# Splitting q and k of a latent-attention encoder into hi and lo parts when they are projected, not when they are read back

## The reference

```python
h = rmsnorm(x, norm_mix)
qa, ka, va, ga, cq, ckv, kr, gb = split(h @ w_in)
ya = window_attention(qa, ka, va, sink) * silu(ga)      # 8 heads, |t-s| <= 128
q = rmsnorm(cq, q_a_norm) @ w_uq                        # 384 -> 8 heads x (64 nope + 32 rope)
kv = rmsnorm(ckv, kv_a_norm) @ w_ukv                    # 256 -> 8 heads x (64 k_nope + 64 v)
q_rope, k_rope = apply_rope(q[..., 64:]), apply_rope(kr)   # k_rope is shared by the heads
scores = (q_nope . k_nope + q_rope . k_rope) * 96 ** -0.5
yb = softmax(scores) @ v * silu(gb)                     # dense, 8 heads, 1024 x 1024
out = rmsnorm(x + concat(ya, yb) @ w_out, final_norm)
```

## Time and profile before

| | |
|---|---|
| median of 3 runs | 620.34 us (619.05 to 620.73) |
| the profiled execution | 619.11 us |
| its span in the trace | 617.3 us |
| PE busy | 605.8 us (98%) |
| weight loads busy | 494.8 us (80%) |
| DVE, ACT, POOL busy | 452.2, 358.4, 320.8 us |
| DMA | 86.36 MB, mean 140 GB/s |
| clock granted to PE, mean over the span | 0.996 |

### The profile page before, as it was taken

One profiled execution on the slowest core, in us unless ns is written; L12 is line 12 of the kernel. 1 busy time (PEld: TensorE's weight loads), 2 busy tenths in 40 slices (PEclk: granted clock), 3 DMA queues, 4 the chain that ended last, 5 costly groups with the idle time before them and its releaser, 6 DMA issues.

```text
span 617.3 us, 9331 instructions
## 1 busy us (share of the span) xinstructions
PE 605.8 (98%) x3180; PEld 494.8 (80%) x3180; DVE 452.2 (73%) x863; ACT 358.4 (58%) x762; POOL 320.8 (52%) x303
## 2 busy tenths in 40 slices
PE   8999998999999999999999999999999999999996
PEld 7888886888888888888887777777777777888885
DVE  5774862534444439989999798988989898789684
ACT  6643431223333228778886787878787788633563
POOL 4611604404656532535537777886887789510701
PEclk9999998999999999999999999999999999999999
DMA  7696457385776620101006633324323423499043
GB/s 252 187 282 210 127 171 252 136 295 170 237 252 227 221 68 2 35 2 35 1 27 152 199 89 74 70 65 90 77 61 78 103 85 138 159 349 343 1 153 121
DMA packets 59089, 86.36 MB, mean 140 GB/s; under 512 B 6617, under 2 KB 32737, under 8 KB 58913
## 3 DMA queue, kind: packets, MB, share of 16 engines
q1 hardware_dynamic: 58880, 85.48, 44.9%
q10 hardware_dynamic: 160, 0.27, 0.1%
HBM read 51.26 MB, written 24.77 MB: 123 GB/s over the span
## 4 chain that ended last, share of the span: by engine, by line
PE 82%; DMA 6%; DVE 5%; ACT 2%; SPq 1%; issue 1%; POOL 1%; DVEq 0%; ACTq 0%
PE ps L1662 14%; PE ps L1664 14%; PE ps L1663 14%; PE ps L1932 10%; PE ps L1950 5%; PE ps L1949 5%; PE ps L1869 5%; PE ps L1864 5%; PE ps L1834 3%; PE ps L1884 2%; DMA lat_scratch<-lat_b 2%; PE ps L1844 2%; DMA x_in<-x 2%; PE ps L1821 2%; PE ps L1820 2%; PE ps L1845 1%
## 5 line engine op out<-in xcount | busy, mean ns | idle before, releaser
L1516 DVE TENSOR_TENSOR pT_lo<-ps,pT_hi 128x512 fp32r<-128x512 f32 x128 | 88.2, 691 | 16.4 <-ACT pT_hi L1105 16.4
L1105 ACT ACTIVATE pT_hi<-ps 128x512 fp32r<-128x512 f32 x128 | 76.0, 596 | 37.0 <-PE ps L1932 36.7
L810 POOL TENSOR_SCALAR p_b<-p_b,stat 128x1024 f32<-128x1024 f32 x64 | 71.9, 1124 | 36.6 <-DVE stat L1511 36.6
L1662 PE MATMUL ps<-hT_hi,w_hi 128*128 128x512 f32 x208 | 84.0, 404 | 0.0
L1664 PE MATMUL ps<-hT_hi,w_lo 128*128 128x512 f32 x208 | 81.4, 391 | 0.0
L1663 PE MATMUL ps<-hT_lo,w_hi 128*128 128x512 f32 x208 | 81.1, 390 | 0.0
L1932 PE MATMUL ps<-ident,p_b 128*128 128x128 f32 x512 | 78.1, 275 | 0.2
L1506 DVE TENSOR_REDUCE stat<-ps 128x1 f32<-128x1024 f32 x64 | 77.7, 1215 | 0.7 <-PE ps L1884 0.6
L1932 PEld LDWEIGHTS ps<-ident,p_b 128*128 128x128 f32 x512 | 60.9, 140 | 21.2 <-issue 7.8
L1094 ACT ACTIVATE p_b<-ps,stat 128x1024 f32<-128x1024 f32 x64 | 71.2, 1113 | 6.4 <-DVE stat L1506 2.5
L1949 PE MATMUL ps<-pT_hi,vB 128*128 128x512 f32 x128 | 55.3, 432 | 0.0
(11 more groups left out here) (219 smaller groups left out, 1476.7 us busy)
## 6 DMA issues: line engine op xcount, KB each, us to landing
w_raw<-w_in SPq DMA_DIRECT2D x13, 512.0 KB, 4.7
x_in<-x SPq DMA_DIRECT2D x8, 512.0 KB, 3.9
wt_raw<-w_out SPq DMA_DIRECT2D x8, 512.0 KB, 4.3
t_scratch<-wt_hi SPq DMA_DIRECT2D x16, 256.0 KB, 2.5
t_scratch<-wt_lo SPq DMA_DIRECT2D x16, 256.0 KB, 2.8
q<-q_h SPq DMA_DIRECT2D x16, 256.0 KB, 3.7
wn_raw<-w_in SPq DMA_DIRECT2D x8, 336.0 KB, 3.7
lat_scratch<-lat_b SPq DMA_DIRECT2D x32, 80.0 KB, 2.2
```

What stands on the lines that cost most here:

```text
L810: nc.gpsimd.tensor_scalar(p_b[:, (U + 1) % 4, :], p_b[:, (U + 1) % 4, :], r_b[:, U % 4:U % 4 + 1], 0.5, ALU.mult, ALU.mult).then_inc(s_bp, 1)
L1105: nc.scalar.activation(pT_hi[:, 1 - G % 2, 4 * a:4 * a + 4, U % 4 * P:(U % 4 + 1) * P], ps[:, 4 + a, :].rearrange("p (k c) -> p k c", c=P) ...
L1516: nc.vector.tensor_tensor(pT_lo[at_], ps[:, 4 + a, :].rearrange("p (k c) -> p k c", c=P), f(pT_hi[at_]), ALU.subtract).then_inc(s_bTl, 1)
L1662: nc.tensor.matmul(o, a_hi, b_hi, start=first, stop=False, skip_group_check=goes_on)
```

## The change

- **Up projections.** Every job but v now has two copies: ACT writes `stage` (hi), DVE writes `stage_lo` (lo = value minus hi), and SP stores both to separate halves of the scratch tensors. The jobs kr take four DMAs, since their rows are also interleaved. `s_upd` counts the lo copies, in the order of the jobs, and it is what the later job of the same bank waits for. The rope jobs r write their products and sums into `r_tmp`; ACT takes hi from there and DVE lo. `stage_lo[2]` and `stage_lo[3]` lie over `lat_b`, so DVE waits there for the last latents' store.
- **Last latents.** `rope_k` now takes blocks 0 to 4 after block 5, and 5 to 7 after block 7; ACT waits for it before block 6's square. Only the first half of `r_q` is loaded ahead of the last trip, the other half after `ukv_raw`.
- **Dense attention.** SP loads hi and lo rows from DRAM straight into `q_1`, `q_2`, `k_1`, `k_2`, `q_c` and `k_c`. All splits of q and k on POOL and DVE, and all copies of rows within SBUF, are gone; POOL still splits v. Loads of head h wait until head h-2 has been scored.
- `sums_wt(0)` on POOL waits until all stores of the up projections have landed, since `wt_sum` lies over `stage_lo`.

Cut to its core:

```diff
-        stage = at("stage", 89, [P, 4, HALF])
+        stage = at("stage", 89, [P, 4, HALF], F32R)
+        stage_lo = [at(f"stage_lo{i}", kb, [P, HALF], F32R) for i, kb in enumerate((113, 205, 142.5, 144.5))]
...
         def wait_up_copied(eng, j):
...
+            eng.wait_ge(s_upd, j + 1)
+        def stored(i, j):
+            dmas = {"kr": 4, "v": 1}
+            return 16 * sum(dmas.get(UP[k][0], 2) for k in range(i, j, 4))
...
-            sp.dma_start(r_q[:, :, :], rope_q).then_inc(s_rq, 16)
+            sp.dma_start(r_q[:, :, 0:HALF], rope_q[:, :, 0:HALF]).then_inc(s_rq, 16)
             move_lat(NT - 1)
             sp.dma_start(ukv_raw[:, :, :, :],
                          w_ukv.rearrange("(k p) (h c) -> p k h c", p=P, c=P)).then_inc(s_ukvi, 16)
+            sp.dma_start(r_q[:, :, HALF:SEQ], rope_q[:, :, HALF:SEQ]).then_inc(s_ukvi, 16)
...
+                for part in range(1 if kind == "v" else 2):
+                    if part == 0 and kind != "v":
+                        sp.wait_ge(s_upa, hi_count(j))
+                    else:
+                        sp.wait_ge(s_upd, j + 1)
+                    src = f(stage[:, j % 4, :] if part == 0 else stage_lo[j % 4][:, :])
...
+            sp.wait_ge(s_ws, REP * (W_UNITS - 1))
+            load_q(0, s_qk0)
...
+            load_k(0, s_qk0)
             sp.dma_start(v_raw[:, :, 0:HD], v_all[:, :, 0:HD]).then_inc(s_v0, 16)
...
+            load_q_c(0, s_qc0)
+            load_q(1, s_qk[1])
+            load_k(1, s_qk[1])
...
             for h in range(2, HEADS):
-                load_qk(h)
-                copy_rows(h)
+                sp.wait_ge(s_bs, NT * (h - 1))
+                load_q(h, s_qk[h % 2])
+                load_k(h, s_qk[h % 2])
+                load_q_c(h, s_qk[h % 2])
...
-                if t == NT - 2:
+                if t == NT - 3:
                     dve.wait_ge(s_small, 32)
-                    rope_k(slice(0, NT - 2))
-            rope_k(slice(NT - 2, NT))
+                    rope_k(slice(0, NT - 3))
+            rope_k(slice(NT - 3, NT))
             lat_lo(NT - 2)
             lat_lo(NT - 1)
...
-                    nc.vector.tensor_tensor(stage[:, (j - 1) % 4, :], r_tmp[:, 0, :], r_tmp[:, 1, :],
-                                            ALU.subtract)
...
+                    for i in (j - 1, j):
+                        dve.wait_ge(s_upa, hi_count(i))
+                        wait_slot(dve, i)
+                        nc.vector.tensor_tensor(stage_lo[i % 4][:, :], r_tmp[:, 2 * (i - j + 1), :], f(stage[:, i % 4, :]),
+                                                ALU.subtract).then_inc(s_upd, 1)
...
+                    if kind == "q":
+                        nc.vector.scalar_tensor_tensor(out=lo, in0=raw, scalar=B_SCALE, in1=hi, op0=ALU.mult,
+                                                       op1=ALU.subtract).then_inc(s_upd, 1)
+                    else:
+                        nc.vector.tensor_tensor(lo, raw, hi, ALU.subtract).then_inc(s_upd, 1)
```

More of the change, by code:

```diff
@@ new lines, in load_k @@
+            def load_k(h, done):
+                hp, rows = h % 2, slice(h * HD, (h + 1) * HD)
+                sp.dma_start(f(k_1[0:HD, hp, :]), k_scr[0, rows, :]).then_inc(done, 16)
+                for part in range(2):
+                    sp.dma_start(f(k_2[HD * (1 - part):HD * (2 - part), hp, :]), k_scr[part, rows, :]).then_inc(done, 16)
+                if h < 2:
+                    for i in range(2):
+                        sp.dma_start(f(k_1[HD + i * ROPE:QK + i * ROPE, hp, :]),
+                                     kr_scr[0].rearrange("p t c -> (p t) c")).then_inc(done, 16)
```

266 lines of the change are left out of this document (91 added, 175 removed).

## The result

The changed kernel takes 627.35 us (median of 4 runs, 625.72 to 629.03), the kernel before 620.34 (619.05 to 620.73): a ratio of 1.011, 95% interval 1.009 to 1.014. It is slower by 7 us. The forecast was 622.8 with a range of 617.5 to 626.0: the direction was right, the size was not. The profiled execution of the changed kernel took 625.72 us with a span of 623.8, against a span of 617.3 before: 6.5 us more.

A forecast was written before the change was run, and what follows sets the result against it. PE, busy 98% of the span, was taken as the bound. Stores +1.7, clock +1.8 and dense start -0.35 summed to +3.15 us, the latents' -0.85 being used up; forecast 622.8 us, between 622.3 and 623.5, range 617.5 to 626.

The forecast's parts named there:

- the start of the dense attention: Dense attention's start: PE's 0.35 us wait for POOL behind the head 0 split goes, -0.35 us.
- the time at which the stores of the second rotated pair begin: Up projections: the second rope pair's first hi part was put at 119.0, after a gap in the stores.
- The removed work in the dense attention: Dense attention: POOL's dropped splits and copies lie beside a PE with a regular period, so 0 us gained.
- so by about 332 … I count no wait: Dense start: head 0's k loads land by about 332, PE needs them at 335.74; q_c lands by 336.
- The last latents: Before job 8: a shorter store-to-load trip, 4.6 us, starts job 8 at 98.5, not 99.35: -0.85 us.
- The doubled stores: At `gated(0)`: 14.5 MB queued ahead delay job 28's copy, so it starts at 137.1, not 135.39: +1.7 us.
- The clock: Behind the wait at `gated(0)`: PE's idle time brings one stretch at 1.2 GHz, +1.8 us.
- The one ending faster: Up projections: stores keep up at 390 GB/s without a gap, `gated(0)` starts 2.7 us earlier, 617.3; chance 0.17.
- a sign of being wrong: Stores: the forecast is wrong if they move at 390 GB/s.
- The rival with waits in more places: Stores at 340 GB/s, `q_c` of head 0 late, or stretched rope pairs making jobs 12 and 20 wait: 626; chance 0.13.

The follow-up runs named there:

- the freed trip alone: Kernel before with half of the rope table's load put behind the weights and k's rotation one tile earlier, nothing else: 621.3 us, ratio 1.002.
- The old-trip run: Changed kernel with the whole rope table again ahead of the last latents' load and k's rotation one tile later: 628.12 us, ratio 1.014.
- the run with v first: Changed kernel with the load of v for the first dense head issued ahead of the five k loads: 625.68 us, ratio 1.009.
- the last version with turns: Changed kernel with last v jobs' banks moved, v loaded first, rotated-q banks freed early, and k and v jobs taking turns: 620.76 us, ratio 1.0013.
- the run with other banks: Changed kernel with the last two v jobs of the up projections in PSUM banks 0 and 1, not 6 and 7: 622.08 us, ratio 1.004.

## Why the prediction was wrong

**The mechanism was the forecast's, two terms of its sum were not.** It gave +3.15 us; the trace has +6.5. The steps that failed are the start of the dense attention, which came out 2.05 us dearer, and the time at which the stores of the second rotated pair begin, which came 1.5 us later.

- *The removed work in the dense attention, 0.* Right. From the first dense scores to the end both traces have 281.5 us, with 56 us less on POOL.
- *The start of the dense attention, -0.35.* Wrong, by 2.05 us. PE's wait for POOL did go, and the step "so by about 332 … I count no wait" looked at k and q_c alone. The step left out that v of head 0, the first load on SP in the earlier trace rows, now stands behind five loads of k, and that ACT's hi part of v stands ahead of the copies that PE's last window products need. It cost +1.70 over the stretch, 1.47 of which came back with one line moved. The rule for each moved step (what is queued behind it, and who waits for that) had been applied to k and not to what k was put in front of.
- *The last latents, -0.85.* Half right, and used up as forecast. Job 8 started at 99.04, not 98.5 (99.35 before). The trip took 5.39 us from store to load (88.33 to 93.72), not the 4.6 taken as a middle. One trace does not settle this: with half of the rope table ahead the trip took 3.2 to 5.8 us in the traces here, with all of it 4.8 to 5.9. Counted from the first up projection the latents' load was issued at 10.6 us here (9.7 to 11.6 in the traces with the new trip) and at 11.7 before (10.8 to 12.5 with the old one), which is near the gain forecast. In the kernel before, the freed trip alone won nothing (ratio 1.002, interval from 1.000 to 1.004); its trace has the first stores later by 1.4 us. The bounds were added up slightly wrong: 88.8 + 3.95 + 4.63 is 97.4, not 97.2, and nothing hangs on it.
- *The doubled stores, +1.7.* The term that decided, right in kind and too small: +3.2. PE came to `gated(0)` at 135.12 and waited 3.47 us, for a v copy behind stores, as the working had it. The first store of the second rotated pair came at 120.47, not 119.0, and from there on the working holds: `gated(0)` comes 18.1 us later in both, at 137.1 and at 138.59. So the 1.5 us lie ahead of that store, and the rows name two causes. One is the pair itself: DVE's products for it began only at 115.94, behind the lo part of job 11, whose hi part had waited for a store of a job kr, and the first sum took 1.33 us, not 0.69. The other is the bytes ahead. At 374 GB/s they were to be gone by 117.5; they kept the engines busy until 120.2, because 106 to 116 ran at 309 GB/s only. There SP takes 3.7 us (109.69 to 113.37) to issue the eight stores of the jobs kr, of 32 KB each, and the share falls to 0.35 at 112 to 114. The sum had counted the bytes of kr and not its eight issues. Since the gap was still there, but only some 1 us long (120.3 to 121.3), an earlier pair alone would have won at most this 1 us. No run here changes the stores of kr, so how much of the 1.5 us is theirs stays open. The old-trip run shows that the pair is the point that counts: the wait was 3.45 us there too, with job 20 at 124.81, 3.6 us later.
- *The clock, +1.8.* Right: +1.68, and gone with spare matmuls in the wait. That the clock held behind job 8 in the profiled execution was luck: it did so after a wait of 2.62 us, and in the run with v first it fell in both places. Two of the changed kernel's four runs took 629 us at a mean clock of 0.992 to 0.994 and two 625.7 at 0.996 to 0.997, which fits a second stretch in the longer ones. But a stretch is worth 1.7 us and the runs are 3.2 apart, and only one of the four has a trace, so the rest of that difference stays open.
- *The rivals.* The one ending faster asked for 390 GB/s without a gap. That rate came over 126 to 136 and was named as a sign of being wrong; it was not one, because the average over 96 to 136 was 343. DMA: Bandwidth & Descriptors of the Trainium skill measured 425 GB/s for 16 MB on one core; no 10 us stretch read here went above 391. The rival with waits in more places, 626 at a chance of 0.13, came nearest, and had named a wait at job 20 (1.03 us came) and a late load at the dense start, though q_c's, not v's.
- *The range.* Its upper end, 626.0, took in one more mishap only. It left out that each further wait of more than 2 us may bring 1.7 us of half clock with it, which makes the slow side longer than the fast side.

The median is 1.6 us above the changed kernel's profiled execution, as the kernel before's is 1.2 above its own; the forecast of 622.8 took in about half of such a gap.

## What to carry to other kernels

Where a change doubles the bytes of stores beside an engine that has no slack, don't ask whether the bytes fit in the whole stage: find the last point at which producer and stores start together, and count bytes and work from there to the buffer that is waited for. Look first at which buffer that is: naming two other PSUM banks gave back 4.8 of 7 us by the ratios, with the stores untouched. Count the issues of small stores beside their bytes (read from the trace here, not tested). And for every load that is put earlier in a queue, write down the load that it now precedes and who waits for that one.

## What was not expected of the hardware

- *Idle time and clock do not map one to one.* Behind job 8 the clock fell after waits of 2.16 us (the last version with turns), 2.42, 2.49, 2.50 (the trip alone) and six from 3.06 to 4.45; it held after 1.24, 1.62, 1.84, 2.60, 2.62, 2.66 and once after 3.20 (the run with other banks). In other places it fell after 2.55, 2.84 and 3.45 to 4.14 and held after 1.74 and less. The row of the first of these:

```profile
96.00:106.00 10.00, 7.84 (x29) 6.21 (x28) 8.28 (x12) 1.34 (x2) 5.50 (x6) 0.83 1.06 362
```

  Whether a wait of 2.2 to 3.2 us costs another 1.7 us could not be told from its length; PE had been busy throughout 80 to 96 in all of these runs. What decides it stays open.
- *A store's issue time on SP varies with what is queued.* For the same 256 KB it was 0.64 us in the k stretch, 0.46 with half of the bytes in every second store, and 0.32 when SP itself had waited.
- *Stores reached 390 GB/s* over 10 us at a DMA share of 1.03, more than the 374 of the earlier trace rows. Loads and stores together made 316 to 357.
- *From issue to landing is no measure of a store here.* With a load of 0.5 MB behind them the four q stores took 8.0 us in the median from issue to landing, with it ahead 5.0. But SP could issue the last of them 3.1 us behind the latents' load instead of 6.7, and counted from that load it landed 0.3 to 0.6 us sooner, not later. A later load still held them up: its 0.5 MB ahead would be 1.4 us at 374 GB/s (an estimate).
- *Small stores left the engines idle here.* Eight of 32 KB took SP 3.7 us to issue, 0.42 to 0.44 us each, and at 112 to 114 us the DMA share was 0.35.
